# Keys requested ahead of values, four gathers moved into the experts' phase, semaphores cleared one phase later, no drain of GpSimd at a block's end

## The reference: what is computed

```
mod = silu(c) @ W_mod + b_mod                    # shift1, scale1, gate1, shift2, scale2, gate2
h = rms_norm(x) * (1 + scale1) + shift1
p = h @ W_in
m = [rwkv7(p) | chunked gMLP(p) | stick-breaking attention(p)]
x = x + gate1 * (m @ W_out)
h2 = rms_norm(x) * (1 + scale2) + shift2
x = x + gate2 * moe(h2)                          # top-1 group of 4, then top-2 experts inside it
y = rms_norm(x)
```

```
z = q @ k_all.T / 8 + bias;   A[t,s] = sigmoid(z[t,s]) * prod_{s<j<t} (1 - sigmoid(z[t,j]))
out = A @ v_all
```

## Time and profile before

| | |
|---|---|
| median of 3 runs | 1554.95 us (1553.19 to 1558.05) |
| the profiled execution | 1558.52 us |
| its span, first to last instruction | 1556.8 us |
| mean granted TensorE clock | 0.939 |
| TensorE busy | 1343.5 us (86%) |
| VectorE busy | 624.2 us (40%) |
| ScalarE busy | 424.2 us (27%) |
| GpSimd busy | 134.2 us (9%) |
| paged attention | 665.9 to 821.9 us |
| experts | 1168.5 to 1498.7 us |
| combine | 1498.7 to 1555.8 us |

### The profile page before, as it was taken

One profiled execution on the slowest core, in us unless ns is written; L12 is line 12 of the kernel. 1 busy time (PEld: TensorE's weight loads), 2 busy tenths in 40 slices (PEclk: granted clock), 3 DMA queues, 4 the chain that ended last, 5 costly groups with the idle time before them and its releaser, 6 DMA issues. The chain is left out here.

```text
span 1556.8 us, 29218 instructions
## 1 busy us (share of the span) xinstructions
PE 1343.5 (86%) x10641; PEld 771.0 (50%) x10641; DVE 624.2 (40%) x1214; ACT 424.2 (27%) x860; POOL 134.2 (9%) x338
## 2 busy tenths in 40 slices
PE   4999899989999999978777899879971999999945
PEld 2564555445353535345546788734431555455512
DVE  3202537613626271843332466523345222222217
ACT  3101134113636372734331232301120111111113
POOL 0100120001101010100000000040001111111031
PEclk9999999999999999979987999979995899999978
DMA  9202122721010100346743000071102768956775
GB/s 352 88 0 74 30 86 95 272 84 42 1 42 1 42 1 20 104 162 201 247 146 123 17 4 4 3 211 57 41 34 77 271 219 300 339 162 243 279 252 197
DMA packets 92403, 191.68 MB, mean 123 GB/s; under 512 B 18539, under 2 KB 41586, under 8 KB 87059
## 3 DMA queue, kind: packets, MB, share of 16 engines
q1 hardware_dynamic: 78900, 158.09, 29.8%
q0 software_dynamic: 6256, 20.71, 3.8%
q10 hardware_dynamic: 7152, 11.55, 2.3%
HBM read 163.01 MB, written 27.31 MB: 122 GB/s over the span
## 5 line engine op out<-in xcount | busy, mean ns | idle before, releaser
L2720 PE MATMUL ex_ps_g<-all_mT,ex_xt 128*64 128x256 f32 x1344 | 157.6, 387 | 5.0 <-DMA all_mT<-in_exp_wu 3.5
L1699 PE MATMUL at_ps_z<-all_hT,mix_v_g 128*128 128x363 f32 (+1 forms) x384 | 121.1, 474 | 4.4 <-PEq L105 4.4
L2333 PE MATMUL op_ps_o<-all_hT,op_m_t 128*128 128x512 f32 x256 | 115.9, 609 | 7.9 <-POOL op_m_t L2313 7.9
L2720 PEld LDWEIGHTS ex_ps_g<-all_mT,ex_xt 128*64 128x64 f32 x1344 | 94.3, 139 | 54.9 <-DMA all_mT<-in_exp_wu 5.8
L576 PE MATMUL rp_ps<-all_hT,mix_rp_w 128*128 128x384 f32 (+1 forms) x336 | 109.4, 482 | 4.1 <-PEq L105 4.1
L1848 DVE TENSOR_SCALAR at_zc<-at_ps_z,at_bias 128x512 f32<-128x512 f32 (+3 forms) x96 | 54.5, 613 | 135.0 <-PE at_ps_z L1715 134.2
L1699 PEld LDWEIGHTS at_ps_z<-all_hT,mix_v_g 128*128 128x128 f32 x384 | 73.2, 192 | 51.0 <-issue 10.0
L341 PE MATMUL fr_big<-all_mT,all_hT 128*128 128x256 f32 (+3 forms) x288 | 94.9, 493 | 3.0 <-DVE all_hT L394 3.0
L576 PEld LDWEIGHTS rp_ps<-all_hT,mix_rp_w 128*128 128x128 f32 x336 | 63.9, 194 | 50.9 <-issue 16.3
L2739 PE MATMUL ex_ps_y<-all_hT,ex_hid_T 128*64 128x512 f32 x336 | 80.5, 600 | 3.8 <-issue 1.6
L2333 PEld LDWEIGHTS op_ps_o<-all_hT,op_m_t 128*128 128x128 f32 x256 | 48.8, 195 | 66.2 <-issue 57.8
(11 more groups left out here) (478 smaller groups left out, 2033.7 us busy)
## 6 DMA issues: line engine op xcount, KB each, us to landing
all_mT<-in_exp_wg SPq DMA_DIRECT2D x34, 512.0 KB, 6.1
all_mT<-in_exp_wu SPq DMA_DIRECT2D x34, 512.0 KB, 7.5
all_hT<-in_exp_wd SPq DMA_DIRECT2D x17, 1024.0 KB, 7.8
all_hT<-in_cache_k SPq DMA_DIRECT2D x64, 256.0 KB, 4.0
sa_v<-in_cache_v SPq DMA_DIRECT2D x64, 256.0 KB, 4.6
slot_rows<-ex_y ACTq DMA_DIRECT2D x84, 128.0 KB, 5.7
mix_v_g<-in_w_mod SPq DMA_DIRECT2D x8, 1024.0 KB, 4.8
rp_w_mod<-in_w_mod SPq DMA_DIRECT2D x8, 1024.0 KB, 5.7
```

The costliest lines, as they stand in the source:

```text
L1699: last = nc.tensor.matmul(third(x_, c), w[:, x_, k, :], hT[:, k, lo:hi], start=(k == 0), stop=(k == KT - 1))
L2333: last = nc.tensor.matmul(ps_o[0:m, u, lo:lo + 512], m_t[:, u, k, 0:m], w[:, k, lo:lo + 512], start=(k == 0), stop=(k == KT - 1))
L2720: final = nc.tensor.matmul(ps_g[rows, u, 0:DE], xt[:, k, HALVES[u]], w1[:, u, x_, k, :], start=(k == 0), stop=(k == KT - 1))
```

## The change

It has four parts.

1. `sampled_attention`: SyncE's order becomes values 0, keys 2, values 1; then twice in a loop keys 3, values 2, keys 4, values 3 (and keys 5, values 4, keys 6, values 5); then keys 7, values 6, values 7. Each item reads its own page numbers.
2. `Phase`: on leaving a phase its semaphores are only noted in `Phase.passed`. The next phase's block clears them ahead of its engines' programs (GpSimd drains and clears), without a barrier behind it. After the last phase there is a barrier, one clear and a barrier.
3. Every block is opened with `no_gpsimd_drain=True`: GpSimd does not drain at its end.
4. The gathers of tiles 0 and 1 (two each) are issued by GpSimd at the end of its program in `experts`, once ScalarE's stores and SyncE's zeros have landed. `combine` issues the other fourteen. The semaphores of the gathers and `final_rows` belong to the outermost scope.

```diff
@@ class Phase
+    passed = []
     def __exit__(self, *_):
-        if self.semaphores:
-            self.nc.clear_and_free_semaphores(self.semaphores)
-            self.nc.all_engine_barrier()
+        self.passed.extend(self.semaphores)
         self.ctx.close()
+    def block(self):
+        self.clear_passed()
+        return self.nc.Block(no_gpsimd_drain=True)
+    def clear_passed(self):
+        if self.passed:
+            self.nc.clear_and_free_semaphores(list(self.passed))
+            self.passed.clear()
@@ each of the nine phases
-        with nc.Block() as block:
+        with ph.block() as block:
@@ def sampled_attention, SyncE
-                def load_values(b, u, pages):
+                def load_keys(b, u):
+                    wait_apart(sp, g["turned"], b * NPAGE + NPAGE, g["passed"])
+                    load_pages(sp, T["cache_k"], k[:, u, :, :], pages_of(sp, table, b), k_loaded[u])
+
+                def load_values(b, u):
                     wait_apart(sp, g["values_done"], b + 1, g["passed"])
-                    load_pages(sp, T["cache_v"], v[:, u, :, :], pages, v_loaded[u])
-
-                def load(b, u):
-
-                    wait_apart(sp, g["turned"], b * NPAGE + NPAGE, g["passed"])
-                    pages = pages_of(sp, table, b)
-                    load_pages(sp, T["cache_k"], k[:, u, :, :], pages, k_loaded[u])
-                    load_values(b, u, pages)
-
-                for b in range(2):
-                    load_values(b, b, pages_of(sp, table, b))
-                with sp.Fori(1, SB // 2) as i:
-                    for u in range(2):
-                        load(i * 2 + u, u)
+                    load_pages(sp, T["cache_v"], v[:, u, :, :], pages_of(sp, table, b), v_loaded[u])
+
+                load_values(0, 0)
+                load_keys(2, 0)
+                load_values(1, 1)
+                with sp.Fori(1, SB // 2 - 1) as i:
+                    load_keys(i * 2 + 1, 1)
+                    load_values(i * 2, 0)
+                    load_keys(i * 2 + 2, 0)
+                    load_values(i * 2 + 1, 1)
+                load_keys(SB - 1, 1)
+                load_values(SB - 2, 0)
+                load_values(SB - 1, 1)
@@ def experts, GpSimd
                 gather(last)
+                pool.wait_ge(s["all_stored"], 2)
+                pool.wait_ge(zeros_stored, (ROUNDS - 1) * 16)
+                gather_rows(nc, keep, slot_rows, range(GATHERED_FIRST))
@@ new, ahead of combine
+GATHERED_FIRST = 2
+def token_rows(keep, n):
+    of_tile = lambda t, at: t[:, :, :].rearrange("p k t -> p (k t)")[:, at * 2 * D:(at + 1) * 2 * D].rearrange("p (c d) -> p c d", c=2)
+    return of_tile(keep["mT"], n) if n < 4 else of_tile(keep["hT"], n - 4) if n < NT else keep["final_rows"][:, :, :]
+
+def gather_rows(nc, keep, slot_rows, tiles):
+    for n in tiles:
+        m = rows_of(n)
+        for c in range(2):
+            nc.gpsimd.indirect_dma_start(token_rows(keep, n)[0:m, c, :], None, slot_rows, bass.IndirectOffsetOnAxis(
+                ap=keep["slots"][0:m, n * 2 + c:n * 2 + c + 1], axis=0)).then_inc(keep["gathered"][n], 16)
@@ def combine, GpSimd
-                for n in range(NT + 1):
-                    m = rows_of(n)
-                    for c in range(2):
-                        nc.gpsimd.indirect_dma_start(rows_at(n)[0:m, c, :], None, slot_rows, bass.IndirectOffsetOnAxis(
-                            ap=slots[0:m, n * 2 + c:n * 2 + c + 1], axis=0)).then_inc(gathered[n], 16)
+                gather_rows(nc, keep, slot_rows, range(GATHERED_FIRST, NT + 1))
@@ def build
         out_project(nc, T, keep, mod_rows, h2_rows)
+        keep["final_rows"], keep["gathered"] = whole.sb("final_rows", [P, 2, D]), [whole.sem(f"gathered{n}") for n in range(NT + 1)]
         experts(nc, T, keep, mod_rows, h2_rows, slot_rows)
         combine(nc, T, keep, slot_rows)
+    nc.all_engine_barrier()
+    whole.clear_passed()
+    nc.all_engine_barrier()
```

More of the change, by code:

```diff
@@ L2945, in combine @@
     with Phase(nc, "cb") as ph:
-        flat = lambda t: t[:, :, :].rearrange("p k t -> p (k t)")[:, 0:8 * D].rearrange("p (n c d) -> p n c d", c=2, d=D)
-        early, late, final_rows = flat(keep["mT"]), flat(keep["hT"]), ph.sb("final_rows", [P, 2, D])
-        rows_at = lambda n: early[:, n] if n < 4 else late[:, n - 4] if n < NT else final_rows[:, :, :]
+        rows_at = lambda n: token_rows(keep, n)
         diag = ph.sb("diag", [P, 4, 2, P])
@@ L2955, in combine @@
         s = {x_: ph.sem(x_) for x_ in names.split()}
-        gathered = [ph.sem(f"gathered{n}") for n in range(NT + 1)]
+        gathered = keep["gathered"]
         stored = [ph.sem(f"stored{u}") for u in range(2)]
         y_tiles = T["y_prompt"].rearrange("(n p) d -> n p d", p=P)
-        with nc.Block() as block:
+        with ph.block() as block:
             @block.gpsimd
             def _(pool):
-                for n in range(NT + 1):
-                    m = rows_of(n)
-                    for c in range(2):
-                        nc.gpsimd.indirect_dma_start(rows_at(n)[0:m, c, :], None, slot_rows, bass.IndirectOffsetOnAxis(
-                            ap=slots[0:m, n * 2 + c:n * 2 + c + 1], axis=0)).then_inc(gathered[n], 16)
+                gather_rows(nc, keep, slot_rows, range(GATHERED_FIRST, NT + 1))
             @block.sync
@@ L3059, in build @@
     keep = {}
+    Phase.passed = []
     mod_rows = scratch("mod_rows", [SB + 1, 6 * D])
```

## The result

The changed kernel takes 1544.4 us (median of 6 runs, 1540.5 to 1548.8) against 1556.5 of the kernel before in the same comparison: a ratio of 0.9924, 95% interval 0.9907 to 0.9942, 12.1 us faster. The forecast was 1551.5, from 1546.0 to 1556.5: sign right, size too small by far.

The account below looks back on a forecast made before the run. TensorE was busy 86% of the 1556.8 us span, so only idle time between matmuls could go. Terms -0.2 - 4.97 - 0.1 + 1.9 = -3.4 us gave 1555.1 for the profiled execution, 1551.5 at the median; range 1546 to 1556.5.

Parts of the forecast that it names:

- the first term, the keys at -0.2 us: Paged attention: keys ahead of values moves TensorE's waits from five places to three, their sum staying 14 to 15 us; -0.2 us.
- The item: SyncE's loop in the paged attention: reading eight page numbers and issuing eight loads takes 9.55 us, for keys and values.
- The prediction's own bound: Paged attention, keys' term: with items of 9.2 us K7 comes 2.8 earlier, with 10.0 us 3.6 later.
- either way: TensorE's clock after each shortened idle stretch may fall either way, 1.1 us a time, making the likeliest case 1547.5 to 1555.5.
- Rival B: Paged attention: SyncE isn't the bound, 14.8 us of waits go and three sequences run faster; another -18, 1533.5; chance 0.06.
- Clears, -4.97: Phase ends: clears moved into the next phase take clear and barrier off the path; -4.97 us, bounds 4.0 and 5.5.
- The experts, forecast -0.9: Experts' phase, from one block's release to the next: forecast to become 0.9 us shorter.
- Kernel's end, -0.1: After the last phase: two clears with a barrier each become barrier, clear, barrier; 0.1 us less.
- Combine, +1.9: Last phase: the clear's drain waits for the four moved gathers, delaying the third tile's rows and the end; +1.9 us.
- Rival A: Last phase: the clear's drain doesn't wait for landings, so the end comes 1.0 us earlier; -6.3 in sum, 1548.7; chance 0.20.

Follow-up runs that it names:

- the five traces named above: Traces of the changed kernel, keys and clears together, no gathers moved, last block drained, and idle transposes in the tail: 1544.4, 1546.2, 1548.0, 1544.0, 1544.4 us.
- f3_no_clears: Changed kernel without its second part, clears and second barriers as before: 1557.0 us in 12 runs, ratio 0.9996 against the kernel before.

## Why the prediction failed

**The step that failed is the first term, the keys at -0.2 us.** Alone they bring 6.7 (4.5 to 8.7). The mechanism was right: SyncE's issue becomes the bound, the waits stand ahead of sequences 5 to 7, and the read-once kernel confirms it. The size was off, in two places that the traces show and in a rest that they don't explain.

- *The item.* With 9.55 us, and 0.3 for the loop's turn, K7's first load was to come 117.9 us behind the phase's start. In the keys-only kernel eight items took 42.1 to 117.1: 9.37 each. The loads took 3.95, as assumed, the reads 5.4, and no loop's turn shows. From K7's first load to the transposes it took 8.4 us and not 9.3. Sequence 7 began at 125.5 instead of 127.4: 2.0 us won where 0.2 was forecast. The prediction's own bound had said it: items of 9.2 give 2.8. A term that is a difference of two long chains wants eight items measured, not one.
- *The clock.* It was put at "either way" in the range, and at nothing in the term. From sequence 7 to the release it took 28.5 us before, 27.9 with keys alone, 26.3 in the changed kernel, with 13, 10 and 7 us of low clock. The length of the last wait doesn't order these (3.60, 0.27, 1.50 us). In the first 40 us the clock fell for 3.4 us twice instead of 13.7 at once, which makes 3 us, in all of the five traces named above, but not with keys alone, where that start has 23.9 us of low clock against 20.5 before. So the keys' part had no clock of one direction: in its own phase it won 2.6 us alone, and 5.8 in company of the clears (155.5 with clears alone, 149.8 with both). Filling TensorE's gaps brought the clock back in the tail and, in part, at the start, so idling matters in both; why it fell less in one kernel than in the other isn't shown.

Rival B, which had the waits gone and cheaper sequences after them, was the right picture of a kernel one step further. That its 1533.5 is so near to what reading once gives (1532.6) is in part luck: B had 18 us in this phase, and the trace has 13.

**Clears, -4.97**: right in size by time (-6.1, interval 3.1 to 9.0). The traces have more in the phases than barriers: in four traces with second barriers the chunks take 195.5 to 203.2 us (mean 198.9), in twelve without 192.6 to 198.2 (194.8), 4.1 less where 1.04 was counted, with 29 and 24 us of low clock. Since the four are spread over 8 us, it isn't shown that the other 3 us belong to the clears. The experts, forecast -0.9, are 1.05 shorter in the same means.

**Kernel's end, -0.1**: wrong, +1.3. The barrier put ahead of the last clear has a drain of GpSimd of 1.21 us, on the path. It was short with the block's drain kept, and short too where a clear's drain came first, without any block drain; so what costs is this order at the end. Why a barrier's drain takes so long there is open.

**Combine, +1.9**: from the last zeros to the last block's release both traces take 61.08 us, so the term is 0.0. With the end, 1.3 stand where 1.8 were forecast, but that nearness is luck: both terms are wrong. The clear's drain was taken for one that lasts until the landing, from two rows of the block's own drain. It is another kind: the clear's ended with the gather's busy time, and the third tile's rows weren't late. The Trainium skill (PSUM — Partial Sum Buffer, Engine vs sequencer instructions) says a drain waits for the engine to go fully idle; the trace agrees for this drain (0.07 us behind) and not for the block's (0.8 to 0.9 us behind the landing). Rival A had the mechanism. Of its 1.0 us nothing is seen in this one trace, and 0.7 in the means of eleven. The matmuls ahead of the rows brought the first product to 3.7 us behind them.

**The sum again.** The keys brought 6.5 us more than forecast and the clears 1.1, the combine's 1.9 didn't come, and the end took 1.4 more: 8.1 of the 8.7 us between forecast and result. That it closes so well says little, since the parts don't add up elsewhere.

**What stays open.** Keys 6.7 won, gathers 1.6 lost, both together 0.6 won. The difference lies in phases that no part touches, with the clock low for 20 to 37 us in the same chunks. The recorded runs say how much the clock can hold of it. Among the runs of one kernel the time falls by 1.0 us for each 0.001 of mean granted clock (all 16 kernels taken together; the runs spread by 1.9 us about that line). The means are 0.9393 before, 0.9415 for keys alone, 0.9403 for the clears, 0.9387 for the gathers, 0.9377 for f3_no_clears. At one and the same clock, as an estimate, the keys would be worth 3.6 us in place of 5.7 (mean against mean), the clears 6.4, the gathers -0.8, and keys and gathers together 1.4, nearer to the 2.8 of their sum. So some 2 us of the keys' gain went with the clock. What sets this clock for a kernel, so that even 12 runs keep it, no experiment here told, and the worth of one part, even at an interval of 2 us, holds only for the company it was timed in.

## What to carry to other kernels

Where one queue issues two kinds of load, put the kind that is waited for first, then count the issue's own instructions: once the order is right its length is the bound, and reading eight numbers once instead of twice was worth as much as the whole change. Before an idle gap of TensorE is called harmless, look at what its next matmuls cost: a few idle matmuls in it gave back 0.5 to 3 us in a phase. Ask what a drain waits for before it is moved or left out: GpSimd's drains here ended with the busy time, or 0.8 us and more behind the landing, or took 1.2 us with everything landed. A single profile of each kernel tells where waits are, but not, at 0.3%, what they are worth; untouched phases differ by up to 8 us.

## What the hardware showed unexpectedly

- GpSimd's drain ahead of a semaphore clear ended 0.07 us behind the last gather's busy time in the changed kernel (0.12 with the gathers alone). The drain at a block's end lasted until 0.8 to 0.9 us behind the landing before, and 1.65 in the kernel with the last block drained.
- Where the first drain behind a last block without drain was a barrier's, it took 1.21 us on GpSimd (1.53 with no gathers moved), though the last gather had landed 26 us earlier (1512.3, drain at 1538.24). Where it was a clear's, it took 0.07 us, and with the block's drain in place the barrier's took 0.05.
- 64 matmuls of 128x128 on 16 columns took 1.94 us at a granted clock of 1.00 and 3.61 at 0.50, the latter behind 3.55 and 1.60 us of idling.
- In one pair of traces the order of two loads that nobody waits for went with a start of the third sequence 2.8 us later and a lower clock, 0.74 instead of 0.79; the same order as in the changed kernel had the late start too in four other kernels (43.0 to 44.2 us).
